# First feed-forward's output: the last three weight units by row tile in place of two, and the first tile's transposes inside the second tile's last unit

## What is computed

```python
        h = rmsnorm(x, g_ff_pre[l])
        y = jnp.square(jax.nn.relu(h @ w_ff1[l])) @ w_ff2[l]     # 1024 -> 4096 -> 1024
        x = x + rmsnorm(y, g_ff_post[l])
    return x
# and the second block begins with
    h = rms_norm(x, norm_mix_g)
    proj = h @ w_in                                              # akv, iq, aq, ... are its columns
```

## Time and profile before

| | |
|---|---|
| median of three runs | 899.44 us (899.38 to 900.24) |
| the profiled execution | 900.26 us |
| its span in the profile | 898.4 us |
| TensorE busy | 884.7 us (98%) |
| VectorE, ScalarE, GpSimd busy | 574.7, 510.9, 88.2 us |

### The profile page before, as it was taken

The page is one execution under the profiler, slowest core; times in us unless marked ns, Lnnn a source line. Parts: engine busy times, 40 slices in busy tenths (PEclk is TensorE's granted clock), DMA queues, the critical chain, the costliest instruction groups (busy, mean ns, idle before and its releaser), DMA issues.

```text
span 898.4 us, 14695 instructions
## 1 busy us (share of the span) xinstructions
PE 884.7 (98%) x5705; PEld 785.2 (87%) x5705; DVE 574.7 (64%) x903; ACT 510.9 (57%) x937; POOL 88.2 (10%) x113
## 2 busy tenths in 40 slices
PE   8999999999999999999999999999999999999998
PEld 8898977888899998887778989988899799998886
DVE  6456656654676664445656999999846576664443
ACT  5566666665666554335558668797255465554330
POOL 0010000010100000001000413341152101000000
PEclk9999999999999999999999999999999999999999
DMA  9856424464455666655364644354430466655552
GB/s 331 301 194 207 141 95 141 138 214 94 146 182 188 194 216 199 201 198 187 115 214 143 190 147 148 126 186 143 116 131 1 126 202 187 190 188 187 189 198 81
DMA packets 110396, 152.24 MB, mean 169 GB/s; under 512 B 6752, under 2 KB 68344, under 8 KB 109944
## 3 DMA queue, kind: packets, MB, share of 16 engines
q1 hardware_dynamic: 110328, 151.31, 52.3%
HBM read 147.99 MB, written 3.30 MB: 168 GB/s over the span
## 4 chain that ended last, share of the span: by engine, by line
issue 47%; PE 38%; DVE 6%; ACT 3%; DMA 2%; POOL 2%; POOLq 1%; DVEq 1%; SPq 0%; ACTq 0%
PE acc L477 5%; PE acc L479 5%; PE acc L478 5%; PE acc L491 4%; PE acc L448 4%; PE acc L489 4%; DVE s_w_lo L420 2%; PE acc L536 1%; PE acc L538 1%; PE acc L537 1%; ACT s_w_hi L414 1%; DMA s_w_raw<-in_w_out 1%; POOLq L676 1%; ACT s_relu_i L1489 1%; POOL s_rstd L677 1%
## 5 line engine op out<-in xcount | busy, mean ns | idle before, releaser
L420 DVE TENSOR_TENSOR s_w_lo<-s_w_raw,s_w_hi 128x2048 fp32r<-128x2048 f32 (+1 forms) x201 | 312.3, 1570 | 169.5 <-ACT s_w_hi L414 169.0
L414 ACT ACTIVATE s_w_hi<-s_w_raw 128x2048 fp32r<-128x2048 f32 (+1 forms) x201 | 263.7, 1333 | 145.9 <-PE acc L479 97.2
L448 PE MATMUL acc<-s_h_lo,s_w_hi 128*128 128x256 f32 (+1 forms) x809 | 221.9, 276 | 0.0
L489 PE MATMUL acc<-s_h_hi,s_w_hi 128*128 128x256 f32 x784 | 218.7, 279 | 0.0
L491 PE MATMUL acc<-s_h_hi,s_w_lo 128*128 128x256 f32 x784 | 217.5, 277 | 0.0
L448 PEld LDWEIGHTS acc<-s_h_lo,s_w_hi 128*128 128x128 f32 x809 | 151.4, 188 | 0.3
L489 PEld LDWEIGHTS acc<-s_h_hi,s_w_hi 128*128 128x128 f32 x784 | 147.3, 188 | 0.3
L491 PEld LDWEIGHTS acc<-s_h_hi,s_w_lo 128*128 128x128 f32 x784 | 147.4, 188 | 0.0
L478 PE MATMUL acc<-s_w_lo,s_hid_hi 128*128 128x512 f32 x224 | 87.2, 389 | 0.0
L477 PE MATMUL acc<-s_w_hi,s_hid_hi 128*128 128x512 f32 x224 | 87.2, 389 | 0.0
L479 PE MATMUL acc<-s_w_hi,s_hid_lo 128*128 128x512 f32 x224 | 87.1, 389 | 0.0
(11 more groups left out here) (333 smaller groups left out, 1454.8 us busy)
## 6 DMA issues: line engine op xcount, KB each, us to landing
s_w_raw<-in_w_in SPq DMA_DIRECT2D x43, 1024.0 KB, 5.2
s_w_raw<-in_w_ff SPq DMA_DIRECT2D x32, 1024.0 KB, 5.3
s_w_raw<-in_w_mlp_up SPq DMA_DIRECT2D x16, 1024.0 KB, 5.5
s_w_raw<-in_w_mlp_down SPq DMA_DIRECT2D x16, 1024.0 KB, 5.0
s_w_raw<-in_w_out SPq DMA_DIRECT2D x8, 1024.0 KB, 5.8
s_w_raw<-in_w_mk SPq DMA_DIRECT2D x4, 1024.0 KB, 5.2
s_w_raw<-in_w_mv SPq DMA_DIRECT2D x4, 1024.0 KB, 5.4
s_w_raw<-in_w_mq SPq DMA_DIRECT2D x4, 1024.0 KB, 5.5
```

What stands on the lines that cost most here:

```text
L414: act.activation(placed(w_hi, u)[:, cs], placed(w_raw, u)[:, cs], ACT.Copy).then_inc(w_hi_done, 4 if q is None else 1)
L420: dve.tensor_tensor(placed(w_lo, u)[:, cs], placed(w_raw, u)[:, cs], placed(w_hi, u)[:, cs].bitcast(F32), ALU.subtract).then_inc(w_lo_done ...
L448: pe.matmul(o[:, ts], wh, lo[:, ts], start=False, stop=False)
L489: pe.matmul(o, wh[:, cs], hi[:, k, :], start=k == 0, stop=False)
```

## The change

`pair_mm` takes a number of units, `count`. For ff2 it is three: units 13, 14 and 15 run for tile 0, then for tile 1. Within tile 1, before the third chunk of unit 15, PE issues the eight transposes of tile 0's normalised rows, which stood at the head of akv before; `head_mm` keeps tile 1's alone. On ACT and DVE the order of the list at the end of ff2 is changed: akv's first unit is split behind tile 0's squares (ACT) and scale (DVE), all four quarters of akv's second unit follow on ACT ahead of tile 0's copies, and on DVE they come in a row behind tile 1's residual add. The second block's feed-forward (`down`) calls the same functions with a count of two and no transposes.

```diff
--- before.py
+++ after.py
@@ -511,7 +511,7 @@
             for i in range(WARM):
                 pe.matmul(aux[3][:, 0:P], junk[:, 0:P], junk[:, P:2 * P], start=True, stop=True)
 
-        def pair_mm(pe, u, hi, lo, fresh=None, before_t=None, within=None):
+        def pair_mm(pe, u, hi, lo, fresh=None, before_t=None, within=None, count=2):
 
             q = units[u]
             if q["before"] is not None:
@@ -522,12 +522,12 @@
                 if before_t is not None:
                     before_t(t)
                 o, ts = acc[q["banks"][t]][:], slice(t * P, (t + 1) * P)
-                for v in (u, u + 1):
+                for v in range(u, u + count):
                     r = units[v]
                     wh, wl = placed(w_hi, v), placed(w_lo, v)
                     for kk in range(4):
                         k, cs = r["k0"] + kk, slice(kk * 512, (kk + 1) * 512)
-                        if within is not None and (v, kk) == (u + 1, 2):
+                        if within is not None and (v, kk) == (u + count - 1, 2):
                             within(t)
                         if t == 0:
                             pe.wait_ge(w_lo_done, 4 * v + kk + 1)
@@ -961,7 +961,7 @@
         DSA = dsa_items()
 
 
-        PAIRS = [of[tag][j] for tag, j in (("out", -2), ("mq", 0), ("mo", -2), ("ff1", 0), ("ff2", -2), ("akv", 0), ("out2", -2),
+        PAIRS = [of[tag][j] for tag, j in (("out", -2), ("mq", 0), ("mo", -2), ("ff1", 0), ("ff2", -3), ("akv", 0), ("out2", -2),
                                            ("up", 0), ("down", -2))]
 
         def wait_tile(eng, u, t):
@@ -969,7 +969,7 @@
             if t == 0:
                 eng.wait_ge(tile_done, PAIRS.index(u) + 1)
             else:
-                eng.wait_ge(unit_done, u + 2)
+                eng.wait_ge(unit_done, u + (3 if u == of["ff2"][-3] else 2))
 
         def half_unit(tag, g):
 
@@ -978,7 +978,7 @@
         def wait_piece(eng, tag, g, t):
 
             if g == 1:
-                wait_tile(eng, of[tag][-2], t)
+                wait_tile(eng, of[tag][-3 if tag == "ff2" else -2], t)
             else:
                 eng.wait_ge(unit_done, half_unit(tag, g) + 1)
 
@@ -1021,19 +1021,18 @@
             for u in of[tag][:-2]:
                 advance_hi(act, u)
             post_stats(act, post, tag, 0)
-            advance_hi(act, last - 1)
-            for t in range(NT):
+            for t in range(NT):
+                if t:
+                    nt_tile_act(act, pre, hi, 0, range(4))
                 post_stats(act, post, tag, 1, [t])
                 if t:
-                    nt_tile_act(act, pre, hi, 0, range(4))
-                    for q in (2, 3):
-                        advance_hi(act, last, q)
                     nt_tile_act(act, pre, hi, 0, range(4, KC))
                 for g in range(2):
                     act.wait_ge(x_done, 2 * NT * TURN[tag] + 2 * t + g + 1)
                     square(act, pre, g, t, x[:, t, g * 512:(g + 1) * 512])
                 if t == 0:
-                    for q in (0, 1):
+                    advance_hi(act, last - 1)
+                    for q in range(4):
                         advance_hi(act, last, q)
             nt_tile_act(act, pre, hi, 1, range(KC))
 
@@ -1044,16 +1043,16 @@
                 advance_lo(dve, u)
             for t in range(NT):
                 post_gain(dve, post, tag, n_load, 0, t)
-            advance_lo(dve, last - 1)
             post_gain(dve, post, tag, n_load, 1, 0)
             post_add(dve, post, 0)
             x_dve_scale(dve, pre, 0)
+            advance_lo(dve, last - 1)
+            nt_tile_dve(dve, pre, hi, lo, 0, range(4))
             post_gain(dve, post, tag, n_load, 1, 1)
-            nt_tile_dve(dve, pre, hi, lo, 0, range(4))
+            nt_tile_dve(dve, pre, hi, lo, 0, range(4, KC))
             post_add(dve, post, 1)
             for q in range(4):
                 advance_lo(dve, last, q)
-                nt_tile_dve(dve, pre, hi, lo, 0, (4 + q,))
             x_dve_scale(dve, pre, 1)
             nt_tile_dve(dve, pre, hi, lo, 1, range(KC))
 
@@ -2580,14 +2579,16 @@
 
             def hidden_mm(tag):
                 hid_hi, hid_lo = HID["ff1" if tag == "ff2" else "up"][0:2]
-                for j in range(len(of[tag]) - 2):
+                count = 3 if tag == "ff2" else 2
+                for j in range(len(of[tag]) - count):
                     if j < len(of[tag]) // 2:
                         pe.wait_ge(hid_lo_done, HB["ff1" if tag == "ff2" else "up"] + 2 * j + 2)
                     mm(tag, j, hi=hid_hi, lo=hid_lo)
-                pair_mm(pe, of[tag][-2], hid_hi, hid_lo)
+                pair_mm(pe, of[tag][-count], hid_hi, hid_lo, count=count,
+                        within=lambda t: nt_tile_pe(pe, xn, 0) if t and tag == "ff2" else None)
 
             def head_mm(tag):
-                pair_mm(pe, of[tag][0], h_hi, h_lo, normed[0], lambda t: nt_tile_pe(pe, xn, t))
+                pair_mm(pe, of[tag][0], h_hi, h_lo, normed[0], lambda t: nt_tile_pe(pe, xn, 1) if t else None)
                 normed[0] += NT * KC
 
             def x_tile(tag, t):
```

## The result

The changed kernel took **901.57 us** (median of 15 runs, 901.08 to 904.35); the kernel before took 900.23 in the 15 runs beside it. The ratio is 1.0020, with a 95% interval of 1.0014 to 1.0027: 1.8 us slower (the two medians are 1.3 us apart). Forecast were 901.4 us and +2.0.

A forecast was written before the change was run, and what follows sets the result against it. PE, busy 98% of the span, was taken as the bound, so only its waits between ff2 and akv could move. Tile 1's first akv matmul going from 432.17 to 434.15 gave 899.44 + 2.0 = 901.4 us, range 900.0 to 902.8.

The forecast's parts named there:

- PE's end of ff2: At ff2's end, tile 0's transposes run inside the last unit without a wait, 0.24 us to spare; PE through at 422.25.
- The load issued: SP's load of akv's second unit goes at 416.09, 5.4 us later, and is usable by ScalarE after 5.6 us.
- ScalarE's queue: ScalarE waits for the load until 421.69, then quarters, tile 0's copies, tile 1's square; akv's first matmul at 425.02.
- VectorE's queue: VectorE reaches tile 1's residual add at 427.75 and the low quarters at 429.08; akv's second unit starts at 429.9.
- Tile 1's scale: In akv, tile 1's scale ready at 432.4, just in time; tile 1's first matmul at 434.15, +2.0 us.
- Nothing behind absorbed the shift: Behind tile 1's start in akv, PE is busy without a gap for 16 us, so no later wait absorbs the shift.
- The total: The whole kernel: median 899.44 us plus 2.0 gives 901.4 us, 0.22% more.
- the load is no wait: Rival: akv's second unit lands soon enough, load 3.5 to 4.8 us, change -0.1 to +1.2, 899.3 to 900.6 us; chance 0.10.
- the clock falls: Rival: PE's clock drops behind the seam's 2.8 and 2.1 us waits, +0.6 to +3.3 on top, 902.0 to 904.7 us; chance 0.05.
- clock full throughout: Sign that the forecast is right: PE's granted clock stays at the full level all through.
- the first of the two places: In the clock rival, akv's first unit: a fall there mostly covered by the wait for low quarters, 0.6 us left.
- the cover works: Rival: tile 0's copies aren't held by the splits at the seam, -1 to -3 us, 896.5 to 898.5; chance 0.05.

The follow-up runs named there:

- late-load kernel: The changed kernel with the load of akv's second unit issued one release later, behind ff2's second-last unit: 904.63 us, ratio 1.0056 to the kernel before.
- the load early: The changed kernel with akv's second unit loaded into the idle buffer foxb, right behind the load of akv's first: 899.77 us, ratio 1.0001 to the kernel before.
- lists-alone kernel: The kernel before with only the change's ScalarE and VectorE lists, PE's order as before: 902.37 us, ratio 1.0034 to the kernel before.
- the transposes at the head: The changed kernel with tile 0's transposes moved back to the head of akv: 901.60 us, ratio 1.0023 to the kernel before.
- last version: The changed kernel with reordered lists, tile 0's copies first, and tile 1's transposes inside akv's second unit: 898.18 us, ratio 0.9982 to the kernel before.
- PE's part alone: The changed kernel with the ScalarE and VectorE lists of the kernel before: 908.44 us, ratio 1.0096 to the kernel before.

## Why the prediction was right

Against the prediction's own steps, with 0.48 added to the times of the trace after:

- PE's end of ff2: forecast 422.25; the transposes ran inside without a wait, as forecast (0.24 us to spare forecast, 0.35 measured), and the last matmul ended at 422.24.
- The load issued: 416.09 forecast, 416.10. Its wait: 5.6 us taken from two rows, **5.31 measured**. The range of the rows (5.40 to 5.71) was a little high; the late-load kernel had 5.06. The step is right, its size 0.3 us too large. The 4.4 us of the Trainium skill (DMA: Bandwidth & Descriptors, "Anatomy of one DMA", a fit for loads issued by GpSimd, where this one is issued by SyncE) were too low by 0.9.
- ScalarE's queue: 421.69, 423.87, 424.92 forecast for the quarters, the copies and the square; 421.41, 423.50, 424.50 measured. Akv's first matmul: 425.02 forecast, 424.64.
- VectorE's queue: the add at 427.75, the low quarters at 429.08 forecast; 427.30 and 428.63. Akv's second unit: 429.9 forecast, 429.37.
- Tile 1's scale: **the step that failed in the sum**. I took 3.47 us from the add to the scale, from tile 0's rows, had the scale ready "just in time" behind the last low quarter and let PE's own matmuls set the transposes. It took 431.10 - 426.82 = 4.28 us, since POOL's operations took longer beside the low quarters (0.94 and 0.79 us, in place of 0.30 and 0.56). VectorE stood idle for 0.45 us, and PE's transposes at 431.91 followed the scale (431.85). That gave back most of what the faster load had saved: tile 1 at 433.99 where 434.15 was forecast, +1.8 in place of +2.0. So the two misses are of opposite sign: 0.5 us early at akv's second unit, 0.4 given back behind it.
- Nothing behind absorbed the shift: D is +1.82, the total's ratio 1.0020.
- The total: that 901.57 us lies 0.2 from the forecast 901.4 is in part luck. The kernel before came out at 900.23 beside it, and not at the 899.44 that I had added to; the change by the medians is +1.3.

The rivals. That the load is no wait: false, the trace shows 1.66 us of it, but its price was right: with the load early the change is worth nothing (1.0001). That the clock falls: **it did fall**, to which I gave 0.05, and "clock full throughout" was a sign that failed. I had read the full level from a row of nines, which didn't show the change's fall of 3 us either; the stretches of the kernel before from 416 to 442 us do have 1.00 each. The trace shows why it didn't matter: the first of the two places, covered by the wait for the low quarters, was the only one it reached, so PE idled for 0.16 us ahead of akv's second unit where I had 2.1. That it stayed covered is luck: in the late-load kernel it cost 0.6 us of D. The Trainium skill (TensorE: Matmul & The Clock Gate, "What's actually happening") says that an idle PE is throttled to half rate. The traces agree in kind: every fall seen here came in or behind a wait of 2.0 to 5.6 us. But the length of one wait doesn't decide: in the profiled executions the clock fell with 2.01 us in the lists-alone kernel (with another 1.00 us shortly ahead of it) and stayed with 2.03 in that with the transposes at the head, most of whose other executions have the lower mean. That the cover works as the lists stand: no; it takes other lists.

What stays open: of the last version's 1.6 us, D has 1.3 and the end of akv 1.4; the rest wasn't traced. Why a wait of 2.0 us brings the clock down in one execution and not in another, of the same kernel too, is open. (The change's D is 0.2 above that of the kernel with the transposes at the head; the load took as much longer, 5.31 us in the one trace and 5.09 in the other.)

## What to carry to other kernels

A unit kept by row tile holds its buffers until the last tile is through: before widening such a group, look which load and which copy wait for those buffers, and what stands behind them in the in-order lists. Work moved under cover helps only if the engine that consumes it gets to it; here PE's transposes were early by 2.5 us and ScalarE was copying weights. Put the copies that the next matmul needs ahead of those it needs later, even if the later ones could start sooner.

## What the runs showed of the hardware

GpSimd's one-column operations took longer beside some of VectorE's work. Where VectorE was idle or read PSUM beside the first of them, they took 0.30 and 0.56 us (424.91 after; 426.52 in the last version, beside `h_lo`). Beside differences of weights, which read two tensors in SBUF, the first took 0.94 us in the change and 1.63 us in the load-early kernel, where it ended 0.2 us behind the last of four quarters (425.97 + 2.50). With PE's part alone it took longest, and it ended 0.2 us behind the difference (417.59 + 2.29) there too:

```profile
418.24 1.81 POOL L675 TENSOR_SCALAR s_stat<-s_stat 128x1 f32<-128x1 f32 x1 [137.60 <-ACT s_junk L644]
```

So tile 1's factor, which these two operations make, came 0.9 us later in the change and 1.3 in the load-early kernel. The Trainium skill (GPSIMD Engine Reference, "Specifications") says that the SBUF interfaces are shared with VectorE, with contention when its instructions have two SBUF inputs. The traces agree in the main; I hadn't looked for it in tile 1's step. No run takes the differences away and leaves the rest as it is, so the cause is read from the times alone. In the last version the first falls beside low chunks read from PSUM; the second ran in part beside a weight difference (from 427.13) and took 0.56 us all the same, so not every overlap costs.
